# Six weight slots in place of four, three units held for both token tiles at the borders of stages, and loops written out, in a two-block transformer kernel

## The chip, the cores and the metric

The program runs on one core of a Trainium2 chip. The metric is the device time of one execution in microseconds (us), the median over several runs. The engines are TensorE (PE, with its weight loads PEld), VectorE (DVE), ScalarE (ACT), GpSimd (POOL) and the queue of SyncE (SP), which only issues transfers here.

## What is computed

256 tokens of width 1024 pass through two transformer blocks, all in float32. Cut to what matters here:

```python
# first block
proj = x @ w_in                                # q, k, v, g, p: 5 x 512 columns
ret  = rms(retention(rope(q), rope(k), v)) * silu(g)
mix  = concat([ret, pool_mixer(p)]) @ w_out
x = layernorm(ALPHA * x + mix)                 # ln1
u = x @ w_up                                   # 2 x 2816 columns
x = layernorm(ALPHA * x + (silu(conv3(gate)) * val) @ w_down)      # ln2
# second block
x = x + 0.5 * rmsnorm(swiglu(rmsnorm(x), ffn1_w_in, ffn1_w_down))
h = rmsnorm(x)                                 # mix_pre
q_a, f_a, i_a, g_a, q_b, k_b, v_b, f_b, gates = split(h @ w_in_2)
y = gate0 * (hgrn2(...) @ w_branch_a) + gate1 * (fox_attention(...) @ w_branch_b)
x = x + rmsnorm(y @ w_out_2)
x = x + rmsnorm(mem_cross_attention(rmsnorm(x), rmsnorm(mem)))
x = x + 0.5 * rmsnorm(swiglu(rmsnorm(x), ffn2_w_in, ffn2_w_down))
```

## The kernel before

**Products.** A weight matrix is streamed from HBM in units of 1 MB: 128 partitions x 2048 float32, which is 4 row chunks of 512 columns. Each float32 number is held as two parts, `high` (rounded by ACT, line 1066) and `rest` (raw minus high, by DVE, line 1538), both fp32r. One product is then three matmuls (high x high, high x rest, rest x high; lines 587 to 589 in `unit`, 624 to 626 in `by_tiles`). There are two token tiles of 128 tokens; a unit has 4 chunks, so 12 matmuls for each tile, 24 in all. There are 180 units, in the order of `BLOCKS`: win1, wout1, up1, down1, upA, downA, win2, brA, brB, mk, wout2, mv, mq, mo, upB, downB. `UNIT[name]` is the number of the first unit of a stage. An up block is two units and fills one PSUM pair; a down stage is 11 units that all add to both pairs.

**Slots.** `raw`, `high` and `rest` have 4 slots of 8 KB per partition each, 96 KB together. Unit u uses slot u % 4. SP loads unit u once DVE has made the rest of unit u - 4 (`unit_rest`); ACT may write `high` of unit u once PE is done with unit u - 4 (`unit_used`). ACT and DVE are in-order queues: where they convert units is fixed in the program by `split_to(n)`, which converts all units below n that aren't converted yet. In the inner blocks it stands at `2 * j + 4`.

**Borders.** At four borders a stage's input comes from a norm over the output of the stage before: wout1 to up1 (called x1 below, a layernorm), down1 to upA (f1, a layernorm), downA to win2 (m2, an RMS norm) and mo to upB (f2, an RMS norm). The last two units of the stage before are multiplied tile by tile (`by_tiles`): first both units for tile 0, which then signals `tile_done`, then both for tile 1, so the norm of tile 0 runs while PE works on tile 1. `first_block` does the same with the first two units of the next stage: it transposes tile 0 on PE in two groups of four (called q0 and q1, line 699, written to PSUM), ACT rounds each group to `xt_high` (line 1080), DVE subtracts to `xt_rest` (line 1556), and PE multiplies tile 0 by both units while the norm of tile 1 is made on DVE and ACT. Then the same for tile 1.

**Names of DVE's steps.** Layernorm: `layer_stats` (line 1644 adds, 1655 and 1657 take the moments, tile 1 needs all of the stage's products) and `layer_norm` (lines 1583, 1663, 1665; with a next gain also 1601); its root is ACT's `layer_root` (line 1117). RMS norm: ACT's `post_norm` takes squares of the stage's output (lines 1151, 1170, 1155, root 1117), DVE's `post_norm` (lines 1583, 1612, 1619, 1601) the rest. At x1 and f1 DVE makes the second `xt_rest` group of tile 0 inside the chain of tile 1, between its moments and its root.

**Loops.** On PE, ACT, DVE and SP, pairs of up blocks, and SP's loads of down stages, are a loop over a register (`turns.loop`). The rest is straight code.

Of the kernel before, what the change touches and what calls it, by code (L numbers as in the profile page):

```python
# [38 lines left out]
P = 128  # L39
# [15 lines left out]
SLOTS = 4  # L55
# [34 lines left out]


class Turns:

    def __init__(self, engine):
        self.engine, self.turn = engine, None

    def __call__(self, n, more):
        return n if self.turn is None or more == 0 else self.turn * more + n  # L100

    @contextmanager
    def loop(self, times, *counts):

        before = [c[0] for c in counts]
        with self.engine.Fori(0, times) as turn:
            self.turn = turn
            yield
            self.turn = None
        for c, n in zip(counts, before):  # L110
            c[0] += (c[0] - n) * (times - 1)

PAIRS = (FB - 1) // 2
CONV_PAIRS = PAIRS - 1


def two_on(key):  # L120
    return key[0], key[1] + 2
# [28 lines left out]
def aux_plan():  # L150
# [36 lines left out]
    for u in range(36):  # L187
        j, last = u // 2, u % 2 == 1
        if u == 1:
            use(("flog", 0))  # L190
# [46 lines left out]
def build(nc, dram, out_dram):  # L237
    ctx = ExitStack()
    with ctx:
# [20 lines left out]
        high = place("high", [P, SLOTS, 4 * NB], F32R, base + 32 * KB)  # L260
        rest = place("rest", [P, SLOTS, 4 * NB], F32R, base + 64 * KB)
# [183 lines left out]
        def _(sync):  # L445
# [3 lines left out]
            turns = Turns(sync)  # L449
# [17 lines left out]
            def load_up(u, w, j):  # L467

                wv = w.rearrange("(k p) n -> p k n", p=P)
                for half in range(2):  # L470
                    k = 4 * half
                    load(u + half, lambda d: [(d.rearrange("p (k g n) -> p k g n", k=4, g=2)[:, :, g, :],
                                               wv[:, k:k + 4, bass.ds(turns(g * FF + 256 * j, 512), 256)])
                                              for g in range(2)])

            def load_down(u, w, i):

                load(u, lambda d: [(d[:, k * D:(k + 1) * D], w[bass.ds(turns((2 * i + k) * P, SLOTS * 2 * P), P), :])
                                   for k in range(2)])

            for name, k in BLOCKS:
# [11 lines left out]
                if name.startswith("up"):  # L493
                    load_up(u, w, 0)
                    with turns.loop(PAIRS):
                        for j in (1, 2):
                            load_up(u + 2 * j, w, j)
                    continue
                if name.startswith("down"):
                    with turns.loop(FB // SLOTS):  # L500
                        for i in range(SLOTS):
                            load_down(u + i, w, i)
                    for i in range(FB // SLOTS * SLOTS, FB):
# [14 lines left out]
        def _(pool):  # L518

            pool.wait_ge(unit_landed[SLOTS - 1], 32)  # L520
# [51 lines left out]
        def _(pe):  # L572
            done = [0]
            turns = Turns(pe)

            def unit(u, products, wait=None):
# [3 lines left out]
                if u:  # L580
                    pe.wait_ge(unit_rest, turns(u + 1, SLOTS))
# [19 lines left out]
            def wait_pair(name, j):  # L601
                n, used = PAIR[name, j]
                if used:
                    pe.wait_ge(pair_taken[n], turns(used, 1))
# [7 lines left out]
            def by_tiles(u, products, before=None, signal=False):  # L612


                for tt in range(TT):
                    for half in range(2):
                        slot = (u + half) % SLOTS
                        if tt == 0:
                            pe.wait_ge(unit_rest, u + half + 1)
                        if before:  # L620
                            before(tt, half)
                        for sh, sr, c, out, first, last in products(half, tt):
# [6 lines left out]
                        elif half == 1 and signal:  # L629
                            mm.then_inc(tile_done, 1)  # L630

            def first_block(name, key, src, ready):

                def before(tt, half):
                    if half == 0:
# [3 lines left out]
                        if tt == 1:  # L639

                            wait_pair(name, 0)
                    wait_taken((key, 2 * tt + half))

                by_tiles(UNIT[name], lambda half, tt: chunk_products(name, 0, half, tt), before)
# [7 lines left out]
            def last_halves(name):  # L652

                by_tiles(UNIT[name] + 2, lambda j, tt: chunk_products(name, j, 1, tt), signal=True)

            def last_block(name, j):
                wait_pair(name, j)
                by_tiles(UNIT[name] + 2 * j, lambda half, tt: chunk_products(name, j, half, tt), signal=True)
# [9 lines left out]
            def down(name, i):  # L668
# [4 lines left out]
                if i < FB - 2:  # L673
                    unit(UNIT[name] + i, [p for kc in (2 * i, 2 * i + 1) for tt in range(TT)
                                          for p in down_products(i, kc, tt)])
                elif i == FB - 1:
                    by_tiles(UNIT[name] + i - 1,
                             lambda half, tt: [p for kc in (2 * (i - 1 + half), 2 * (i - 1 + half) + 1)
                                               for p in down_products(i - 1 + half, kc, tt)], signal=True)

            def aux(key):
# [3 lines left out]
                if used:  # L685
                    more = AUX[two_on(key)][2] - used if turns.turn is not None else 0
                    pe.wait_ge(aux_taken[bank], turns(used, more))
# [96 lines left out]
            def conv_transposes(j):  # L784
                pe.wait_ge(pair_taken[j % 2], turns(taken("up1", j)[1], 1))
# [4 lines left out]
            first_block("up1", "x1", from_x, lambda tt, q: pe.wait_ge(x_ready, x_at("ln1", tt, q)))  # L790
            full_block("up1", 1)
            conv_transposes(0)
            full_block("up1", 2)
            conv_transposes(1)
            with turns.loop(CONV_PAIRS, done):
                for j in (3, 4):
                    full_block("up1", j)
                    conv_transposes(j - 1)
# [7 lines left out]
            def ffn(u_name, d_name, h_name, key, pre):  # L806
                first_block(u_name, key, from_y, lambda tt, q: pe.wait_ge(normed, normed_at(pre, tt, q)))
                with turns.loop(PAIRS, done):
                    for j in (1, 2):
                        full_block(u_name, j)  # L810
                        hidden_transposes(u_name, h_name, j - 1)
# [6 lines left out]
            def hidden_transposes(u_name, h_name, j):  # L818
                n, count = taken(u_name, j)
                pe.wait_ge(pair_taken[n], turns(count, 1))  # L820
# [90 lines left out]
            for u in range(36):  # L911
                j, half = divmod(u, 2)
                if u == 0:
                    first_block("win2", "m2", from_y, lambda tt, q: pe.wait_ge(normed, normed_at("mix_pre", tt, q)))
                if u >= 2:
                    half_block("win2", j, half)
                if u in (1, 2):
                    fox_logits(u - 1)
# [121 lines left out]
        def _(act):  # L1040
# [3 lines left out]
            turns = Turns(act)  # L1044
# [8 lines left out]
            def split_to(n):  # L1053

                while split[0] < min(n, UNIT["end"]):
                    u = split[0]
                    act.wait_ge(unit_landed[u % SLOTS], turns(32 * (u // SLOTS + 1), 32))
                    if u >= SLOTS:
                        act.wait_ge(unit_used, turns(u - SLOTS + 1, SLOTS))
# [9 lines left out]
            def aux(key):  # L1069
                n, bank, _ = AUX[key]  # L1070
                more = AUX[two_on(key)][0] - n if turns.turn is not None else 0
                act.wait_ge(aux_done, turns(n + 1, more))
# [32 lines left out]
            def block_values(name, j):  # L1105
                act.wait_ge(unit_used, turns(filled(name, j), SLOTS))
# [116 lines left out]
            tile_groups("x1", 0)  # L1223
            layer_root("ln1", 1)
# [3 lines left out]
            def conv_values(j):  # L1228

                out = aux(("convg", j))  # L1230
                if j >= 2:
                    act.wait_ge(sem("ffn_rest"), turns(j - 1, 2))
                for c in range(2):
                    f = 2 * j + c
                    act.activation(conv[:, j % 2, c, :], out[:, c * S:(c + 1) * S], ACT.Identity,  # L1235
                                   scale=small["convw"][:, bass.ds(turns(3 * f + 2, 12), 1)],
                                   bias=small["convb"][:, bass.ds(turns(f, 4), 1)]).then_inc(sem("conv_last"), 1)
                act.wait_ge(aux_taken[6], turns(AUX["convg", j][2] + 1, 2))
# [952 lines left out]
```

## Time and profile before

| What | us |
|---|---|
| median of 3 runs | 1156.87 (1154.71 to 1157.2) |
| the profiled execution | 1158.97 |
| its span, first to last instruction | 1157.2 |
| PE busy | 1118.8 (97%) |
| PE weight loads | 933.2 (81%) |
| DVE busy | 690.4 (60%) |
| ACT busy | 562.6 (49%) |
| POOL busy | 42.5 (4%) |

The profile is of one execution. PE is busy in nearly the whole span, so the table tells little by itself; what is to be read is where PE stands still. The clock that TensorE was granted is 1.00 (2.4 GHz) or half of it (1.2 GHz), and its mean over the span is 0.995.

### The profile page before, as it was taken

How to read it: one execution, taken by the hardware profiler on the slowest of the kernel's cores; microseconds unless marked ns; L12 is line 12 of the kernel's file. 1: busy time of each engine (PE TensorE's matmuls, PEld its weight loads, DVE VectorE, ACT ScalarE, POOL GpSimd, SP SyncE). 2: the span in 40 equal slices, each digit the busy share in tenths (PEclk: the TensorE clock that was granted, in tenths of full speed). 3: DMA queues.
4: the chain of work that ended last, by engine and by line, in shares of the span. 5: the costliest groups of instructions: out<-in, count | busy, mean ns of one | idle time of the engine just before them, and what ended most of it. 6: DMA issues, size and time to landing. Idle time of an engine off the chain costs nothing.

```text
span 1157.2 us, 14090 instructions
## 1 busy us (share of the span) xinstructions
PE 1118.8 (97%) x5370; PEld 933.2 (81%) x5370; DVE 690.4 (60%) x682; ACT 562.6 (49%) x645; POOL 42.5 (4%) x50
## 2 busy tenths in 40 slices
PE   7999999999899999999999999999999899999997
PEld 5887888888788888878888888888888777888786
DVE  4548566665755545477976765667556347555442
ACT  4463556554363534466545545546355535435342
POOL 1900000000000000000000000010000000000000
PEclk9999999999999999999999999999999989999999
DMA  9645564547376555544543443464546233655530
GB/s 362 214 152 182 183 202 161 200 163 255 124 240 193 169 214 188 204 157 146 182 146 111 144 146 109 146 236 164 198 166 242 85 126 94 216 185 177 206 121 37
DMA packets 126145, 201.01 MB, mean 174 GB/s; under 512 B 6304, under 2 KB 74048, under 8 KB 125968
## 3 DMA queue, kind: packets, MB, share of 16 engines
q1 hardware_dynamic: 122624, 187.78, 47.3%
q0 software_dynamic: 3472, 12.55, 3.2%
q8 instruction: 34, 0.56, 0.2%
q14 instruction: 15, 0.12, 0.0%
HBM read 199.26 MB, written 1.05 MB: 173 GB/s over the span
## 4 chain that ended last, share of the span: by engine, by line
PE 91%; DVE 4%; ACT 2%; issue 2%; DMA 0%; SPq 0%; DVEq 0%; ACTq 0%
PE ps L587 24%; PE ps L589 24%; PE ps L588 24%; PE ps L699 4%; PE ps L624 3%; PE ps L625 3%; PE ps L626 3%; PE ps L857 2%; ACT high L1066 1%; DVE rest L1538 1%; PE ps L985 1%; PE ps L998 1%; DVE xt_rest L1556 1%; DMA x<-in_x_dram 0%; ACT xt_high L1080 0%
## 5 line engine op out<-in xcount | busy, mean ns | idle before, releaser
L1538 DVE TENSOR_TENSOR rest<-raw,high 128x2048 fp32r<-128x2048 f32 (+1 forms) x180 | 405.0, 2279 | 177.0 <-ACT high L1066 177.0
L587 PE MATMUL ps<-high,xt_high 128*128 128x512 f32 x928 | 369.7, 398 | 3.7 <-DVE rest L1538 2.1
L1066 ACT ACTIVATE high<-raw 128x2048 fp32r<-128x2048 f32 (+1 forms) x177 | 331.4, 1907 | 73.3 <-PE ps L589 72.5
L589 PE MATMUL ps<-high,xt_rest 128*128 128x512 f32 x928 | 363.8, 392 | 0.0
L588 PE MATMUL ps<-rest,xt_high 128*128 128x512 f32 x928 | 363.0, 391 | 0.0
L587 PEld LDWEIGHTS ps<-high,xt_high 128*128 128x128 f32 x928 | 175.5, 189 | 38.7 <-issue 2.5
L589 PEld LDWEIGHTS ps<-high,xt_rest 128*128 128x128 f32 x928 | 175.2, 189 | 37.6
L588 PEld LDWEIGHTS ps<-rest,xt_high 128*128 128x128 f32 x928 | 175.6, 189 | 34.9
L587 PE MATMUL ps<-high,ht_high 128*128 128x512 f32 x216 | 84.6, 392 | 2.5 <-issue 2.5
L589 PE MATMUL ps<-high,ht_rest 128*128 128x512 f32 x216 | 84.2, 390 | 0.0
L588 PE MATMUL ps<-rest,ht_high 128*128 128x512 f32 x216 | 84.0, 389 | 0.0
L1283 ACT ACTIVATE act<-ps,recips 128x256 f32<-128x256 f32 x44 | 18.5, 471 | 124.5 <-PE ps L589 124.5
L1779 DVE SCALAR_TENSOR_TENSOR hid<-ps,recips,act 128x256 f32<-128x256 f32 x44 | 19.3, 480 | 83.4 <-ACT act L1283 83.4
L1080 ACT ACTIVATE xt_high<-ps 128x512 fp32r<-128x512 f32 x38 | 21.2, 600 | 62.9 <-PE ps L699 62.9
L624 PE MATMUL ps<-high,xt_high 128*128 128x512 f32 x112 | 45.8, 409 | 5.1 <-DVE xt_rest L1556 5.0
L587 PEld LDWEIGHTS ps<-high,ht_high 128*128 128x128 f32 x216 | 40.5, 188 | 11.2 <-issue 3.1
L589 PEld LDWEIGHTS ps<-high,ht_rest 128*128 128x128 f32 x216 | 40.5, 188 | 8.6
L588 PEld LDWEIGHTS ps<-rest,ht_high 128*128 128x128 f32 x216 | 40.6, 188 | 8.3
L625 PE MATMUL ps<-rest,xt_high 128*128 128x512 f32 x112 | 45.1, 403 | 0.0
L626 PE MATMUL ps<-high,xt_rest 128*128 128x512 f32 x112 | 45.0, 402 | 0.0
L1556 DVE TENSOR_TENSOR xt_rest<-ps,xt_high 128x512 fp32r<-128x512 f32 x38 | 24.8, 684 | 21.9 <-ACT xt_high L1080 21.8
L1721 DVE SCALAR_TENSOR_TENSOR conv<-ps,convw,conv 128x255 f32<-128x255 f32 (+1 forms) x44 | 19.2, 478 | 20.7 <-ACT conv L1235 19.4
(304 smaller groups left out, 1168.0 us busy)
## 6 DMA issues: line engine op xcount, KB each, us to landing
raw<-in_w_in_dram SPq DMA_DIRECT2D x92, 512.0 KB, 4.2
raw<-in_ffn_w_in_dram SPq DMA_DIRECT2D x88, 512.0 KB, 4.7
raw<-in_w_up_dram SPq DMA_DIRECT2D x44, 512.0 KB, 4.7
raw<-in_ffn_w_down_dram SPq DMA_DIRECT2D x44, 512.0 KB, 4.1
raw<-in_w_down_dram SPq DMA_DIRECT2D x22, 512.0 KB, 4.7
raw<-in_w_out_dram SPq DMA_DIRECT2D x16, 512.0 KB, 4.3
raw<-in_w_mkv_dram SPq DMA_DIRECT2D x16, 512.0 KB, 5.1
raw<-in_w_branch_a_dram SPq DMA_DIRECT2D x8, 512.0 KB, 3.9
```

The costliest lines, as they stand in the source:

```text
L587: pe.matmul(out, sh, wh, start=first, stop=False)
L588: pe.matmul(out, sh, wr, start=False, stop=False)
L589: mm = pe.matmul(out, sr, wh, start=False, stop=last)
L624: pe.matmul(out, sh, wh, start=first, stop=False)
L625: pe.matmul(out, sh, wr, start=False, stop=False)
L626: mm = pe.matmul(out, sr, wh, start=False, stop=last)
L699: mm = pe.transpose(out[:, n * P:(n + 1) * P], src, ident[:, :])
L857: mm = pe.matmul(out[:, c:c + P // 2], hqk[:, h, t], q, start=True, stop=True)
L1066: act.activation(high[:, u % SLOTS, c], raw[:, u % SLOTS, c], ACT.Copy).then_inc(unit_high, 1)
L1080: act.activation(dst, src, ACT.Copy).then_inc(group_high, 1)
L1538: vec.tensor_tensor(rest[:, slot, c], raw[:, slot, c], high[:, slot, c].bitcast(F32), ALU.subtract).then_inc(sem("lead_rest") if lead else ...
L1556: vec.tensor_tensor(dst_rest, src, dst_high.bitcast(F32), ALU.subtract).then_inc(aux_taken[bank], 1)
```

## The change

`raw` and `rest` now share one place: DVE writes the rest over the raw data. With that there are 6 slots of 16 KB (raw/rest and high), 96 KB as before. A load of unit u now waits until PE is done with unit u - 6. `split_to` stands one unit further ahead (`+ 5`) in the inner blocks. At a border three units (`LEAD = 3`) are held for both tiles, before the border (down stages only) and behind it (`first_units`); at the ends of wout1 and mo it is still two. All loops over registers are written out. The forget-gate logits of win2 (`fox_logits`) come two units later.

```diff
-SLOTS = 4
+SLOTS = 6
+LEAD = 3
...
         raw = place("raw", [P, SLOTS, 4 * NB], F32, base)
-        high = place("high", [P, SLOTS, 4 * NB], F32R, base + 32 * KB)
-        rest = place("rest", [P, SLOTS, 4 * NB], F32R, base + 64 * KB)
+        rest = place("rest", [P, SLOTS, 4 * NB], F32R, base)
+        high = place("high", [P, SLOTS, 4 * NB], F32R, base + 48 * KB)
...
-                    sync.wait_ge(unit_rest, turns(u - SLOTS + 1, SLOTS))
+                    sync.wait_ge(unit_used, u - SLOTS + 1)
...
-            def first_block(name, key, src, ready):
+            def first_units(name, key, src, ready):
...
-                by_tiles(UNIT[name], lambda half, tt: chunk_products(name, 0, half, tt), before)
+                by_tiles(UNIT[name], LEAD, lambda n, tt: chunk_products(name, n // 2, n % 2, tt), before)
+                half_block(name, 1, 1)
...
-                if i < FB - 2:
+                if i < FB - LEAD:
...
-                with turns.loop(PAIRS, done):
-                    for j in (1, 2):
-                        full_block(u_name, j)
-                        hidden_transposes(u_name, h_name, j - 1)
+                hidden_transposes(u_name, h_name, 0)
+                for j in range(2, FB):
+                    full_block(u_name, j)
+                    hidden_transposes(u_name, h_name, j - 1)
...
                 def up_block(j):
-                    split_to(UNIT[u_name] + 2 * j + 4)
+                    split_to(UNIT[u_name] + 2 * j + 5)
...
             post_norm("ffn1_post", "downA", 0)
             first_group("m2")
+            split_to(UNIT["win2"] + LEAD)
             post_norm("ffn1_post", "downA", 1)
             other_groups("m2")
...
             layer_norm("ln1", 0)
-            tile_groups("x1", 0, halves_=(0,))
+            tile_groups("x1", 0)
+            split_to(UNIT["up1"] + LEAD)
             layer_stats("wout1", 1)
-            tile_groups("x1", 0, halves_=(1,))
             layer_norm("ln1", 1)
             tile_groups("x1", 1)
```

On DVE at the border x1, from the last step of tile 0's norm to tile 1's, before:

```order
L1665 SCALAR_TENSOR_TENSOR x<-y,recips,gains 128x512
L1556 TENSOR_TENSOR xt_rest<-ps,xt_high 128x4x128
L1644 SCALAR_TENSOR_TENSOR y<-x,ps 128x512 x2
L1655 BN_STATS moments<-y 128x6 x2
L1657 BN_AGGR meanvar<-moments 128x2
L1556 TENSOR_TENSOR xt_rest<-ps,xt_high 128x4x128
L1583 RECIPROCAL recips<-roots 128x1
```

and in the changed kernel (line numbers shift; 1619 is the old 1665, 1493 the old 1538, 1598 the old 1644):

```order
L1619 SCALAR_TENSOR_TENSOR x<-y,recips,gains 128x512
L1510 TENSOR_TENSOR xt_rest<-ps,xt_high 128x4x128 x2
L1493 TENSOR_TENSOR rest<-raw,high 128x2048
L1598 SCALAR_TENSOR_TENSOR y<-x,ps 128x512 x2
L1609 BN_STATS moments<-y 128x6 x2
L1611 BN_AGGR meanvar<-moments 128x2
L1537 RECIPROCAL recips<-roots 128x1
```

The second `xt_rest` group moved ahead of tile 1's first step, and one conversion of 128x2048, that of the third unit, now stands between them.

On ACT at the border m2, from the rounding of q0 of tile 0, before:

```order
L1117 ACTIVATE roots<-sums,eps 128x1
L1080 ACTIVATE xt_high<-ps 128x4x128
L1151 ACTIVATE y,eps<-ps 128x512
L1170 ACTIVATE y,sums<-ps 128x512
L1155 ACTIVATE eps<-eps 128x1
L1117 ACTIVATE roots<-sums,eps 128x1
L1080 ACTIVATE xt_high<-ps 128x4x128 x3
```

and in the changed kernel:

```order
L1076 ACTIVATE roots<-sums,eps 128x1
L1039 ACTIVATE xt_high<-ps 128x4x128
L1026 ACTIVATE high<-raw 128x2048
L1110 ACTIVATE y,eps<-ps 128x512
L1129 ACTIVATE y,sums<-ps 128x512
L1114 ACTIVATE eps<-eps 128x1
L1076 ACTIVATE roots<-sums,eps 128x1
L1039 ACTIVATE xt_high<-ps 128x4x128 x3
L1026 ACTIVATE high<-raw 128x2048
```

ACT's half of the third unit's conversion (`high<-raw`) stands behind q0 and ahead of tile 1's squares, and q1 of tile 0 (the first of the last `xt_high` three) is still behind those squares. At f2 the order is the same; at x1 and f1 both groups of tile 0 come first, then the conversion.

## Rows read from the trace of the kernel before

**Rows 1.** Page: costliest groups (busy, mean ns, idle before) and one DMA issue (KB, us to landing).
```profile
L1538 DVE TENSOR_TENSOR rest<-raw,high 128x2048 fp32r<-128x2048 f32 (+1 forms) x180 | 405.0, 2279 | 177.0 <-ACT high L1066 177.0
...
L1066 ACT ACTIVATE high<-raw 128x2048 fp32r<-128x2048 f32 (+1 forms) x177 | 331.4, 1907 | 73.3 <-PE ps L589 72.5
...
raw<-in_w_up_dram SPq DMA_DIRECT2D x44, 512.0 KB, 4.7
```

**Rows 2.** Windows, end of the old stage to tile 1's first product: x1, f1, m2, f2.
```profile
106.06:116.47 10.41, 8.14 (x41) 6.08 (x40) 8.94 (x16) 2.96 (x6) 1.05 (x2) 1.00 0.03 9
301.26:313.99 12.73, 9.80 (x41) 7.34 (x41) 11.58 (x19) 2.59 (x6) 1.75 (x4) 0.87 0.04 6
494.85:505.60 10.75, 8.08 (x41) 6.21 (x41) 8.61 (x15) 4.20 (x11) 1.06 (x2) 1.00 0.09 29
959.13:968.82 9.69, 8.09 (x41) 6.14 (x40) 7.49 (x12) 3.58 (x10) 0.00 (x0) 1.00 0.00 0
```

The columns are the window and its length, then busy us and count of PE, PEld, DVE, ACT and POOL, the granted clock, the DMA share and GB/s.

**Rows 3.** Timeline of PE at x1, tile 0 (start, us, instruction, idle before).
```profile
107.33 0.66 PE L699 MATMUL ps<-ident,x 128*128 128x128 f32 x4 [0.68 <-DVE x L1665]
108.07 0.50 PE L624 MATMUL ps<-high,xt_high 128*128 128x512 f32 x1
```

**Rows 4.** Timeline of DVE at x1: tile 1's chain, first and last.
```profile
107.93 1.27 DVE L1644 SCALAR_TENSOR_TENSOR y<-x,ps 128x512 f32<-128x512 f32 x2
...
113.74 0.75 DVE L1665 SCALAR_TENSOR_TENSOR x<-y,recips,gains 128x512 f32<-128x512 f32 x1
```

**Rows 5.** Timeline of PE at f1, tile 0.
```profile
304.13 0.65 PE L699 MATMUL ps<-ident,y 128*128 128x128 f32 x4 [1.57 <-DVE y L1601]
...
304.73 0.54 PE L624 MATMUL ps<-high,xt_high 128*128 128x512 f32 x1
```

**Rows 6.** Timeline of DVE at f1: tile 1's chain, first and last.
```profile
304.59 1.28 DVE L1644 SCALAR_TENSOR_TENSOR y<-x,ps 128x512 f32<-128x512 f32 x2
...
312.05 0.69 DVE L1601 TENSOR_TENSOR y<-x,gains 128x512 f32<-128x512 f32 x1
```

**Rows 7.** Timeline of PE at m2: tile 0's first product, tile 1's transposes.
```profile
497.88 0.50 PE L624 MATMUL ps<-high,xt_high 128*128 128x512 f32 x1
...
503.50 1.07 PE L699 MATMUL ps<-ident,y 128*128 128x128 f32 x8
```

**Rows 8.** Timeline of PE at f2: tile 0's first product.
```profile
961.14 0.50 PE L624 MATMUL ps<-high,xt_high 128*128 128x512 f32 x1
```

**Rows 9.** Timeline of ACT at f2: tile 1's squares, then q1 of tile 0.
```profile
960.26 0.59 ACT L1151 ACTIVATE y<-ps 128x512 f32<-128x512 f32 x1
...
961.94 0.58 ACT L1080 ACTIVATE xt_high<-ps 128x512 fp32r<-128x512 f32 x1
```

**Rows 10.** Timeline of DVE at f2: q1 of tile 0, tile 1's chain, first and last.
```profile
962.55 0.69 DVE L1556 TENSOR_TENSOR xt_rest<-ps,xt_high 128x512 fp32r<-128x512 f32 x1 [1.46 <-ACT xt_high L1080]
963.16 0.15 DVE L1583 RECIPROCAL recips<-roots 128x1 f32<-128x1 f32 x1
...
967.11 0.69 DVE L1601 TENSOR_TENSOR y<-x,gains 128x512 f32<-128x512 f32 x1
```

**Rows 11.** Timeline of PE inside mo, ahead of a stretch at clock 0.5.
```profile
923.17 1.06 PE L699 MATMUL ps<-ident,mo 128*128 128x128 f32 x8 [0.90 <-issue]
925.86 0.47 PE L587 MATMUL ps<-high,xt_high 128*128 128x512 f32 x1 [1.62 <-DVE xt_rest L1556]
```

**Rows 12.** Timeline of PE in upA: transposes behind three blocks one after another.
```profile
341.81 0.60 PE L699 MATMUL ps<-ident,hid 128*128 128x128 f32 x4
...
353.16 0.60 PE L699 MATMUL ps<-ident,hid 128*128 128x128 f32 x4
...
364.53 0.60 PE L699 MATMUL ps<-ident,hid 128*128 128x128 f32 x4
```

**Rows 13.** Timeline of PE: first product of downA, behind the loop.
```profile
434.40 0.47 PE L587 MATMUL ps<-high,ht_high 128*128 128x512 f32 x1 [1.09 <-issue]
```

**Rows 14.** Timeline of DVE at the same place: it empties the last pair.
```profile
433.42 0.88 DVE L1779 SCALAR_TENSOR_TENSOR hid<-ps,recips,act 128x256 f32<-128x256 f32 x2 [4.22 <-ACT act L1283]
```

More of the change, by code:

```diff
@@ L89 @@
 OA_SLOT = {30 + _g: _g for _g in range(4)}
[L92 to L121, printed above, removed]
 def unit_starts():
@@ L493, in _ @@
                 if name.startswith("up"):
[L494 to L497 removed]
+                    for j in range(FB):
+                        load_up(u + 2 * j, w, j)
                     continue
                 if name.startswith("down"):
[L500 to L503, printed above, removed]
+                    for i in range(FB):
                         load_down(u + i, w, i)
@@ L610, in half_block, with by_tiles @@
                 unit(UNIT[name] + 2 * j + half, [tiles[tt][k] for k in range(4) for tt in range(TT)])
-            def by_tiles(u, products, before=None, signal=False):
+            def by_tiles(u, units, products, before=None, signal=False):
                 for tt in range(TT):
-                    for half in range(2):
-                        slot = (u + half) % SLOTS
+                    for n in range(units):
+                        slot = (u + n) % SLOTS
                         if tt == 0:
-                            pe.wait_ge(unit_rest, u + half + 1)
+                            pe.wait_ge(unit_rest, u + n + 1)
                         if before:
-                            before(tt, half)
-                        for sh, sr, c, out, first, last in products(half, tt):
+                            before(tt, n)
+                        for sh, sr, c, out, first, last in products(n, tt):
                             wh, wr = high[:, slot, c:c + NB], rest[:, slot, c:c + NB]
@@ L685, in aux @@
                 if used:
-                    more = AUX[two_on(key)][2] - used if turns.turn is not None else 0
-                    pe.wait_ge(aux_taken[bank], turns(used, more))
+                    pe.wait_ge(aux_taken[bank], used)
                 return ps[:, bank, :]
@@ L1070, in aux @@
                 n, bank, _ = AUX[key]
-                more = AUX[two_on(key)][0] - n if turns.turn is not None else 0
-                act.wait_ge(aux_done, turns(n + 1, more))
+                act.wait_ge(aux_done, n + 1)
                 return ps[:, bank, :]
@@ L1249, in up1_block @@
                     conv_values(j - 1)
-            up1_block(0)
-            up1_block(1)
-            up1_block(2)
-            with turns.loop(CONV_PAIRS, split, steps):
-                up1_block(3)
-                up1_block(4)
-            split_to(UNIT["down1"] + 4)
+            for j in range(FB):
+                up1_block(j)
+            split_to(UNIT["down1"] + 5)
             conv_values(FB - 1)
@@ L1286, in up_block @@
                         hidden_high(j - 1)
-                up_block(0)
-                with turns.loop(PAIRS, split, steps):
-                    up_block(1)
-                    up_block(2)
-                split_to(UNIT[d_name] + 4)
+                for j in range(FB):
+                    up_block(j)
+                split_to(UNIT[d_name] + 5)
                 hidden_high(FB - 1)
@@ L1522, in settle @@
             def settle():
[L1523 removed]
+                vec.wait_ge(mine, steps[0])
             def split_to(n):
@@ L1543, in aux @@
                 n, bank, _ = AUX[key]
-                more = AUX[two_on(key)][0] - n if turns.turn is not None else 0
-                vec.wait_ge(aux_done, turns(n + 1, more))
+                vec.wait_ge(aux_done, n + 1)
                 return ps[:, bank, :]
@@ L1737, in up1_block @@
             def up1_block(j):
-                split_to(UNIT["up1"] + 2 * j + 4)
+                split_to(UNIT["up1"] + 2 * j + 5)
                 if j:
                     conv_values(j - 1)
-            up1_block(0)
-            up1_block(1)
-            up1_block(2)
-            steps_a_turn[0] = 6
-            with turns.loop(CONV_PAIRS, split, steps):
-                up1_block(3)
-                up1_block(4)
-            split_to(UNIT["down1"] + 4)
+            for j in range(FB):
+                up1_block(j)
+            split_to(UNIT["down1"] + 5)
             conv_values(FB - 1)
@@ L1785, in up_block @@
                         hidden_rest(j - 1)
-                up_block(0)
-                steps_a_turn[0] = 2
-                with turns.loop(PAIRS, split, steps, groups, silus):
-                    up_block(1)
-                    up_block(2)
-                split_to(UNIT[d_name] + 4)
+                for j in range(FB):
+                    up_block(j)
+                split_to(UNIT[d_name] + 5)
                 hidden_rest(FB - 1)
```

133 lines of the change are left out of this document (65 added, 68 removed).

## Prediction

> **What bounds the kernel now.** The first view is the page's table of engines: PE is busy for 97% of the span, and the number of matmuls does not change, so all that this change can move is the time in which PE stands still or runs at the lower clock. So the second view is the list of who PE waits for. It holds no row with a weight unit but one at the very start: PE never waits for a conversion in the middle of a stage, and four slots are already enough there. The waits stand at the borders of stages, behind norms, and inside the memory attention. So the third view is the timeline of PE, ACT and DVE at each of the four borders x1, f1, m2 and f2. The windows [rows 2] give the length of each, from the end of the old stage (called T) to tile 1's first product: 10.41, 12.73, 10.75 and 9.69 us, with PE busy for about 8 us of each. The reader is to see that DVE is busy in most of these windows too: in the first for 8.94 of 10.41 us, in the second for 11.58 of 12.73. The border is a chain of norms on DVE with PE as its customer, not the reverse.
>
> **A unit held for both tiles.** Three blocks of an up stage begin 11.35 and 11.37 us apart [rows 12], with four transposes (half of the 1.07 us of eight [rows 7], less their overlap: 0.45); four tile-units lie between, so a unit for one tile is 2.73 us of PE. Tile 0 then covers 8.2 us with three units instead of 5.5. The work is moved and not added. To compare, I let both kernels reach the same point: before, tile 1 starts with two units of tile 0 done, so the third adds 2.73 to its window.
>
> **What stands in tile 1's way.** The third unit has to be converted, and its place is the in-order queues of ACT and DVE ahead of tile 1's norm. ACT takes 1.91 us, DVE 2.28 [rows 1]. Its data is there: the slot was freed six units earlier, and a half of a unit lands in 4.7 us [rows 1]. But ACT comes to it only behind tile 0's `xt_high`, so DVE waits for ACT and then converts, in front of tile 1's chain.
>
> *x1.* T is 106.06. The last steps of tile 0 are as before: wout1 still ends with two units, q1 is transposed at 107.33 and the first product comes at 108.07, 0.74 later [rows 3]. ACT rounds q1 until 108.5, converts until 110.4; DVE converts until about 112.8. Tile 1's chain started at 107.93 before [rows 4], so it is 4.9 late; its last step ended at 113.74 + 0.75 = 114.5, now 119.4, and with 0.74 more tile 1's products start at 120.2, which is T + 14.1. Before, with the third unit added: 10.41 + 2.73 = 13.1. A loss of 1.0.
>
> *f1.* Here down1 ends with three units by tiles, so tile 0's norm starts 2.73 earlier. T is 301.26; the transposes of q1 came at 304.13 [rows 5], T + 2.9, now about T + 0.1. What is left is the way from both transposes to the product: at m2 503.50 to 505.60, so 2.1 [rows 7, 2]. Tile 0 starts at T + 2.1 and not at 304.73, T + 3.5 [rows 5]. ACT is free of `xt_high` at about T + 1.7, converts until T + 3.6, DVE until T + 5.9. Tile 1's chain takes 304.59 to 312.74, 8.15 [rows 6], so it ends at T + 14.0, and the products come at T + 14.8. Before: 12.73 + 2.73 = 15.5. A gain of 0.7.
>
> *m2 and f2.* Here ACT also has q1 of tile 0 behind tile 1's squares. Those take 960.26 to 961.94, 1.68 [rows 9]. From ACT's step behind q0, T + 1.1: 1.9 conversion, 1.7 squares, 0.6 rounding, 0.7 `xt_rest` [rows 10]: q1 is there at T + 6.0. PE wants it one unit behind its first product, which at f2 comes at 961.14, T + 2.0 [rows 8], so at T + 4.8: a new stop of 1.2. Then DVE converts until T + 8.3, its chain takes 963.16 to 967.80, 4.64 [rows 10], and with 0.74 tile 1 starts at T + 13.7. Before, f2: 9.69 + 2.73 = 12.4, a loss of 1.3. m2: tile 0's norm starts 2.73 earlier here too, its first product came at 497.88, T + 3.0 [rows 7], and comes at T + 2.1; but tile 1 starts at T + 13.7 as at f2, against 10.75 + 2.73 = 13.5: a loss of 0.2.
>
> Sum of the orders: 1.0 - 0.7 + 0.2 + 1.3 = 1.8 us of loss. Each border ends with DVE's conversion on the path; the bounds are 0 for it where it should fit into a hole (then the borders give -4.9, below) and its full length with ACT's, as here.
>
> **The clock.** The clock was granted at half in f1's window: its mean is 0.87, so 0.13 x 12.73 = 1.65 us of full-clock work were lost [rows 2]. What PE had done before: it stood from T to 304.73, 3.5 us with eight transposes in between [rows 5]. Inside mo it fell too, behind 922.27 to 925.86, 3.6 us with eight transposes [rows 11]. At m2, with 3.0 us of the same kind, and at x1 and f2, with 2.0, it stayed at 1.00 [rows 2, 3, 7, 8]. In f1 the loss was hidden: tile 1 waited for DVE anyway. Now the large holes lie behind tile 0's three units: at x1 from about 116.4 to 120.2, 3.8 us, at f1 from T + 10.4 to T + 14.8, 4.4 us, each with eight transposes. What follows them is 36 products with nothing to hide the slow ones, so each fall costs 1.65. By the nearest rows both are on the falling side; m2's 3.0 us is not far. I take 0.75 for f1 and 0.6 for x1: 1.35 x 1.65 = 2.2 us, between 0 and 3.3. The Trainium skill, TensorE: Matmul & The Clock Gate, Part 1, says that the lower clock is the default and that activity releases it. By that rule larger holes are a loss in themselves, and the trace agrees: the clock is at 0.5 behind the two longest holes quoted here; without it the sum would be 1.8, with it 4.0.
>
> **Slots, loads, loops.** In mid-stage a load waits for PE to finish unit u - 6 and lands 4.7 us later [rows 1], less than two units of 5.46 on PE; ACT could start on it only once PE had finished unit u - 4 before. So no conversion comes later, and as PE waited for none, none is worth anything earlier: 0. The cover is two units; were it gone, each unit would show its own wait. DVE writes over one of its operands now; no row here shows what that costs at this size. The nearest spread between two conversions of 128x2048 is DVE's 2.28 against ACT's 1.91 us [rows 1], so I bound it by 0.37 us either way at each of the four borders, where alone it is on the path (1.5 in all), and take 0, since operation and sizes stay. Loops: blocks of upA start 11.35 us apart once and 11.37 the next time, and one of these two steps has the loop's turn in it, since a turn is two blocks [rows 12], so a turn costs 0 within 0.02. The logits' move is PE work of the same length: 0.
>
> Sum: 1.8 + 2.2 = 4.0 us. The profiled execution took 1158.97 with a span of 1157.2; it is 2.1 above the median, a little more than one slow stretch of the clock. Added to the median 1156.87: **1160.9**.
>
> **Rivals.**
> *The third unit fits in* (faster). If DVE and ACT had the conversion done in idle time, tile 0's 8.2 us would cover most of tile 1's chain and each border would end on PE alone: T + 2.1 + 8.2 + 2.1 = 12.4. Against 13.1, 15.5, 13.5 and 12.4 that is -0.7 - 3.1 - 1.1 + 0 = -4.9 with f1's and x1's holes gone: 1152.0. For it speaks that tile 1's chain is only 4.6 us long at m2 and f2 [rows 10]; against it the order of the queues, and that DVE has hardly 1.5 us free at x1. It decides where the conversion costs a border less than about 1.2 us. 0.12.
> *Loops cost more than their turns* (no change). Downs start with a wait: 1.09 us at downA [rows 13], of which there are two like it. If that were code being fetched behind the loop, writing it out gives 2.2 us back: 1160.9 - 2.2 = 1158.7. Against it: DVE empties the last pair until 433.42 + 0.88 = 434.30, and the product comes at 434.40 [rows 13, 14]. That explains it whole. The Trainium skill, Runtime: NRT & Kernel Launch, Instruction fetch mechanics, says that a taken branch breaks the sequential prefetch and that kernels prefer full unrolling; by that rule this rival would win, and the trace does not agree, by the turns above. 0.08.
> *No clock falls* (no change). The holes stay but the clock holds: 1156.87 + 1.8 = 1158.7. For it: m2. 0.22.
> *Order and clock as summed*: 0.58, with one fall 1160.3, with both 1162.0.
>
> **Numbers.** 0.2% of 1156.87 is 2.3 us, about what a measurement of this kernel can tell from no change: slower is above 1159.2, faster below 1154.6. The first rival (0.12) is faster, and some 0.04 of the others, where my chains are two or three us too long. The middle two fall mostly within. The range leaves out the first rival and little above both falls: 1154.5 to 1163.5. The likeliest case alone: 1159.3 to 1163.
>
> **What would show it.** In the changed kernel, the conversion (128x2048 on DVE) directly ahead of tile 1's chain at each border; PE waiting 3 to 4 us ahead of tile 1 at x1 and f1 and about 1.2 ahead of the second unit of tile 0 at m2 and f2; tile 0's first product at f1 1.4 earlier; clock 0.5 behind the holes. Wrong would be: DVE finding the third unit converted, ACT reaching it before q0, a wait for a weight unit in mid-stage, or a stop where a loop used to be.

## The result, and the profile after

The changed kernel takes 1170.4 us in the median of 4 runs (1169.04 to 1171.12), the kernel before 1156.94 (1154.71 to 1157.2) beside it: a ratio of 1.0119 (95%: 1.0102 to 1.0137), 13.5 us slower. The sum was 4.0 us. The profiled execution took 1169.95 us with a span of 1167.8 and a mean clock of 0.992.

The page after, parts 1, 3 and 5: engines, one DMA queue, and the two groups that answer to [rows 1].

```profile
PE 1120.2 (96%) x5370; PEld 934.2 (80%) x5370; DVE 688.7 (59%) x682; ACT 561.0 (48%) x645; POOL 42.5 (4%) x50
...
q8 instruction: 43, 0.70, 0.2%
...
L1493 DVE TENSOR_TENSOR rest<-raw,high 128x2048 fp32r<-128x2048 f32 (+1 forms) x180 | 404.9, 2279 | 168.9 <-ACT high L1026 168.8
...
L1026 ACT ACTIVATE high<-raw 128x2048 fp32r<-128x2048 f32 (+1 forms) x177 | 330.9, 1907 | 44.7 <-DMA raw<-in_ffn_w_down_dram 22.3
```

The busy times are within 2 us of those of before, and a conversion that writes over the raw data takes the same 2279 ns. So the loss is idle time and clock. The windows of the four borders after, x1, f1, m2, f2, read as [rows 2]: from the end of the old stage to tile 1's first product.

```profile
104.55:118.86 14.31, 11.15 (x53) 8.65 (x52) 11.25 (x16) 3.89 (x5) 0.53 (x2) 0.96 0.37 124
301.93:316.57 14.64, 10.91 (x53) 8.65 (x52) 11.44 (x17) 3.78 (x5) 1.32 (x3) 0.97 0.38 130
495.89:509.61 13.72, 10.88 (x53) 8.34 (x52) 8.53 (x11) 5.41 (x11) 1.06 (x2) 1.00 0.36 131
968.40:982.12 13.72, 11.09 (x53) 8.32 (x52) 9.69 (x13) 5.42 (x11) 0.00 (x0) 1.00 0.38 127
```

They hold three units of tile 0 now. The prediction had 14.1, 14.8, 13.7 and 13.7. The borders came out as worked out, so most of the missing 9.5 us is elsewhere. It shows in the list of whom PE waits for (us in total, times, the longest):

```profile
...
PE ps L586 <- DVE xt_rest L1510: 6.3, 7, 1.6
PE ps L664 <- DVE y L1555: 4.5, 5, 1.6
PE ps L664 <- DVE flog L1857: 4.3, 1, 4.3
...
PE ps L664 <- DVE x L1619: 3.1, 3, 1.6
...
PE ps L884 <- DVE flog L1934: 1.9, 1, 1.9
```

Two of these rows are of no border: `flog`, the logits of the forget gate in win2, whose move the prediction had at 0. DVE's timeline in that place (start, us, instruction, idle before and its releaser):

```profile
524.67 2.29 DVE L1493 TENSOR_TENSOR rest<-raw,high 128x2048 fp32r<-128x2048 f32 x1
526.88 0.99 DVE L1889 TENSOR_SCALAR he<-ps,lb 128x256 f32<-128x256 f32 x2
533.30 1.00 DVE L1889 TENSOR_SCALAR he<-ps,lb 128x256 f32<-128x256 f32 x2 [5.44 <-PE ps L800]
534.44 0.69 DVE L1897 TENSOR_SCALAR hk<-he 128x1024 f32<-128x1024 f32 x1
...
543.18 0.22 DVE L1854 SCALAR_TENSOR_TENSOR flog<-ps,recips,flb 128x8 f32<-128x8 f32 x2
543.44 0.36 DVE L1857 SCALAR_TENSOR_TENSOR flog<-ps,recips,flog 128x8 f32<-128x8 f32 x2
```

DVE empties two groups of transposed `f` (line 1889). The first pair of steps goes through, the second stands 5.44 us and is released by line 800, which is the last matmul of the *logits*. And PE's:

```profile
525.02 1.09 PE L664 MATMUL ps<-ident,stage 128*128 128x128 f32 x8
525.86 0.48 PE L549 MATMUL ps<-high,xt_high 128*128 128x512 f32 x1
...
543.85 0.74 PE L664 MATMUL ps<-ident,stage 128*128 128x128 f32 x4 [4.34 <-DVE flog L1857]
...
558.87 0.38 PE L884 MATMUL ps<-ident,flog 128*8 128x128 f32 x2 [1.85 <-DVE flog L1934]
```

All eight transposes that DVE wants had been issued at 525.02. What holds DVE back is a count: every group in the four rotating PSUM banks adds 1 to one semaphore, `aux_done`, and a reader of group n waits for n + 1, in the order of `aux_plan`. The logits are one group written in two halves a unit of work apart. Before, its number and both halves came at steps 1 and 2, ahead of the transposes. In the change its number stands at step 3 ahead of those of `f`, but its second half is issued at step 4, behind them. So the second group of `f` is counted as there only when the logits are. DVE is late from then on and comes to `flog` only at 543.18; PE wants that bank for its next transposes and stands 4.34 us. DVE's small subtraction into `flog` (line 1934) is late as well: 1.85 us more. The clock falls behind the longer wait (windows after, columns as above):

```profile
540.00:544.00 4.00, 0.15 (x1) 0.15 (x2) 3.23 (x7) 2.57 (x3) 0.00 (x0) 1.00 0.71 258
544.00:548.00 4.00, 4.00 (x14) 3.23 (x14) 3.97 (x6) 3.04 (x5) 0.00 (x0) 0.57 0.00 0
```

That is 0.43 x 4.00 = 1.7 us, with the two waits 7.9 us, of the 9.5 that the sum missed. That is a reading; the runs below test it.

### The profile page after: what moved, and what is told of

Same layout as the page of the kernel before. It is cut to its first block, busy times and chain, and to the rows that moved or that the text cites. A ratio compares the mean times of both kernels' runs of the same rounds, so it can differ in the third digit from the quotient of the medians.

```text
span 1167.8 us, 13128 instructions
## 1 busy us (share of the span) xinstructions
PE 1120.2 (96%) x5370; PEld 934.2 (80%) x5370; DVE 688.7 (59%) x682; ACT 561.0 (48%) x645; POOL 42.5 (4%) x50
## 4 chain that ended last, share of the span: by engine, by line
PE 88%; DVE 5%; ACT 3%; issue 2%; DMA 0%; SPq 0%; DVEq 0%; ACTq 0%
PE ps L549 22%; PE ps L551 22%; PE ps L550 22%; PE ps L664 4%; PE ps L586 4%; PE ps L587 4%; PE ps L588 4%; PE ps L818 2%; ACT high L1026 1%; DVE rest L1493 1%; PE ps L946 1%; PE ps L959 1%; DMA x<-in_x_dram 0%; ACT xt_high L1039 0%; DVE xt_rest L1510 0%
## 5 line engine op out<-in xcount | busy, mean ns | idle before, releaser
L1493 DVE TENSOR_TENSOR rest<-raw,high 128x2048 fp32r<-128x2048 f32 (+1 forms) x180 | 404.9, 2279 | 168.9 <-ACT high L1026 168.8
L549 PEld LDWEIGHTS ps<-high,xt_high 128*128 128x128 f32 x896 | 169.1, 189 | 37.3 <-issue 2.5
L551 PEld LDWEIGHTS ps<-high,xt_rest 128*128 128x128 f32 x896 | 168.9, 188 | 36.2
L550 PEld LDWEIGHTS ps<-rest,xt_high 128*128 128x128 f32 x896 | 169.4, 189 | 33.5
L549 PE MATMUL ps<-high,ht_high 128*128 128x512 f32 x192 | 75.3, 392 | 2.6 <-issue 2.6
L551 PE MATMUL ps<-high,ht_rest 128*128 128x512 f32 x192 | 74.8, 390 | 0.0
L550 PE MATMUL ps<-rest,ht_high 128*128 128x512 f32 x192 | 74.7, 389 | 0.0
L549 PEld LDWEIGHTS ps<-high,ht_high 128*128 128x128 f32 x192 | 36.0, 188 | 10.5 <-issue 3.2
L551 PEld LDWEIGHTS ps<-high,ht_rest 128*128 128x128 f32 x192 | 36.0, 188 | 7.6
L550 PEld LDWEIGHTS ps<-rest,ht_high 128*128 128x128 f32 x192 | 36.1, 188 | 7.3
L586 PEld LDWEIGHTS ps<-high,xt_high 128*128 128x128 f32 x144 | 28.4, 197 | 14.5 <-DVE xt_rest L1510 4.8
```

The source lines that it names most:

```text
L549: pe.matmul(out, sh, wh, start=first, stop=False)
L550: pe.matmul(out, sh, wr, start=False, stop=False)
L551: mm = pe.matmul(out, sr, wh, start=False, stop=last)
L586: pe.matmul(out, sh, wh, start=first, stop=False)
L1493: vec.tensor_tensor(rest[:, slot, c], raw[:, slot, c], high[:, slot, c].bitcast(F32), ALU.subtract).then_inc(sem("lead_rest") if lead else ...
```

## The experiments

All ten kernels compute the same outputs: only the order of work changes. The first theory: logits about 8 us, borders 4 us with clock, the rest nothing. The rivals: the loops or slots cost, or the borders are worth more than their windows. The kernel before was measured again beside each group of runs, and its median came out between 1156.33 and 1157.3; so a difference of two medians from different groups is good to about 1 us.

**1. Logits moved, in the kernel before.**

```diff
-        if u == 1:
+        if u == 3:
             use(("flog", 0))
...
-                if u in (1, 2):
-                    fox_logits(u - 1)
+                if u in (3, 4):
+                    fox_logits(u - 3)
```

The steps of ACT and DVE that follow come two units later too, as in the change.

> The kernel before with only the logits moved two units later, as the change does it (halves on both sides of the first f transposes), four slots and loops as before. Theory of the count: DVE waits some 5 us for the second half here too, PE waits at the second f transposes and at the flog transposes: 5 to 8 us slower than before, 1162 to 1165. Rival (deeper conversions or slots are the cause): within 1 us of 1157.

Measured: 1163.94 us, ratio 1.0065 (1.0049 to 1.0081), +7.6 us. Its list of waits has the row that was to be explained:

```profile
PE ps L699 <- DVE flog L1910: 4.3, 1, 4.3
...
PE ps L923 <- DVE flog L1987: 1.8, 1, 1.8
```

and DVE stands in the same place, released by the last matmul of the logits (line 839 here):

```profile
529.60 1.00 DVE L1942 TENSOR_SCALAR he<-ps,lb 128x256 f32<-128x256 f32 x2 [6.16 <-PE ps L839]
```

The two waits and the fall of the clock behind them (1.7 us, at 540 to 546) make 7.8. Nothing else was changed, so this edit, in a kernel whose slots, borders and loops are those of before, makes the stop and most of the missing time. Shown.

**2. The halves together, in the changed kernel.**

```diff
-                if u in (3, 4):
-                    fox_logits(u - 3)
+                if u == 3:
+                    fox_logits(0)
+                    fox_logits(1)
```

> The changed kernel with both halves of the forget-gate logits ahead of the first f transposes, not one on each side of them. Theory (order of the count): the signal that a PSUM group is ready is one count for all groups in program order; in the changed kernel the logits' group is numbered ahead of the f transposes but finished one unit behind them, so DVE and ACT, which wait for the transposes' number, wait for the logits too (5.44 us on DVE), come late to the logits' bank and PE stands 4.34 + 1.85 us in the next two places. With both halves ahead these waits and the low clock behind them go: 6 to 8 us less than the changed kernel, 1162 to 1164. Rival (the deeper conversions, one unit further ahead, hold ACT and DVE up in win2): the waits stay, within 1 us of 1170.

Measured: 1166.38 us, ratio 1.0092 (1.0076 to 1.0108), 4.0 less than the change; 6 to 8 had been expected. The stop of 4.34 is gone, so the count was its cause, but less comes back than stop and clock together (6.0). The windows of this kernel around the logits (32 matmuls of 16 and 8 columns, 524.05 to 527.54):

```profile
526.00:530.00 4.00, 4.00 (x28) 3.71 (x28) 3.46 (x5) 0.26 (x1) 0.00 (x0) 0.81 0.64 243
530.00:534.00 4.00, 4.00 (x15) 3.15 (x15) 2.74 (x6) 2.97 (x4) 0.00 (x0) 0.76 0.00 0
```

PE is busy for 4.00 of 4.00 us, and still the clock falls behind the logits: (0.19 + 0.24) x 4.00 = 1.7 us. One repair brought a loss of its own.

**3. Halves apart, numbered and issued behind the transposes.**

```diff
-        if u == 3:
-            use(("flog", 0))
...
                 use((WIN2[j - 1][0] + "T", 2 * ((j - 1) % 2) + g))
+        if u == 3:
+            use(("flog", 0))
```

On PE, the call of `fox_logits` is placed behind the transposes of the same step.

> The changed kernel with the logits numbered and issued behind the first f transposes, one half there and one half a unit later. Theory: the count is in order again, so the 4.34 us wait goes as in the run with both halves together, and as the two halves of small matmuls are a unit apart the clock, which fell behind them there though PE stood nowhere, stays up: 2 us less than that run's 1166.4, 1163.5 to 1165. Rival (the clock fell for another reason, such as its phase): equal to it within 0.8 us.

Measured: 1164.6 us, ratio 1.0064 (1.005 to 1.0078), 5.8 less than the change. No stop at the transposes and no fall behind the logits; but the second wait is now 2.6 us, and the clock falls behind that one:

```profile
PE ps L882 <- DVE flog L1934: 2.6, 1, 2.6
```

The time is in the range that was expected, but not for the reason given there. Against experiment 2 the trace has as many falls of the clock in win2, one, and a second wait that is 0.8 us longer (2.6 for 1.8). What its trace has less is one fall inside mo, where the two programs are alike. That the halves apart are worth 1.8 us is not shown by this run; experiment 10 asks it again.

**4. Logits repaired whole, borders as in the change.** As 3, and DVE's subtraction into `flog` stands ahead of the conversions of its step:

```diff
+                if u == 6:
+                    vec.wait_ge(sem("flog_ln"), 1)
+                    vec.tensor_tensor(flog[:, :, :], flabs[:, :, :], flmin[:, :, :], ALU.subtract).then_inc(sem("flog_ready"), 1)
                 split_to(UNIT["win2"] + u + 5)
```

> The changed kernel with the logits repaired in full (behind the first f transposes, halves a unit apart, small subtraction ahead of the conversion) and the borders left as the change has them. This measures the sum of the prediction by itself: orders at the borders 1.8 us of loss and two clock falls of 1.65 at x1 and f1, 1160 to 1162.5 against 1157 of before. Rival (the four borders cost more than their orders, since the run with the early third unit gained 9.3 us, more than the 6.7 plus 3.3 summed for it at the low end): 1163 or more. Rival (less than predicted): under 1159.

Measured: 1161.41 us, ratio 1.0041 (1.0026 to 1.0057), +4.2 us. This is the kernel that the prediction had summed: 4.0 above the median, and inside its range. PE's waits at the borders are those of the change:

```profile
PE ps L586 <- DVE xt_rest L1510: 6.3, 7, 1.6
PE ps L664 <- DVE y L1555: 4.5, 5, 1.6
...
PE ps L664 <- DVE x L1619: 3.1, 3, 1.6
```

Of `flog` one wait of 0.4 is left.

**5. Loops written out alone, in the kernel before.**

```diff
-                with turns.loop(PAIRS, done):
-                    for j in (1, 2):
-                        full_block(u_name, j)
-                        hidden_transposes(u_name, h_name, j - 1)
+                for j in range(1, FB):
+                    full_block(u_name, j)
+                    hidden_transposes(u_name, h_name, j - 1)
```

and so for every other loop over a register on PE, ACT, DVE and SP.

> The kernel before with all register loops written out and nothing else. Theory: the turns cost nothing before and longer code costs nothing: within 1 us of 1157. Rival (longer code has to be fetched in order and PE or SP waits for it): 1 to 4 us slower. Rival (a loop's turn or end costs time): 1 to 3 us faster, with the waits of 1.1 us ahead of the down stages gone.

Measured: 1157.04 us, ratio 1.0003 (0.9992 to 1.0014). No difference that can be told.

**6. Slots and loops alone.** The change with `LEAD = 2` and the logits in their old place.

> The changed kernel with two units held at the borders and the logits in their old place: what is left is six slots with the rest over the raw data, loads that wait for PE, conversions one unit further ahead, and loops written out. Theory: these parts are worth nothing, within 1.2 us of 1156.3. Rival (writing over an operand or the later loads cost): 1158 or more. Rival (deeper slots help by themselves): 1155 or less.

Measured: 1158.12 us, ratio 1.0006 (0.9997 to 1.0015). Six slots, the rest over the raw data, the split one unit further ahead and the written-out loops together are within what can be measured. The 1158.12 is above what was expected and just inside the rival's "1158 or more", but the kernel before stood at 1157.3 beside it and not at 1156.3: the difference is 0.8 us, at most 1.7 by the interval. No wait for a weight unit is in its list but the one at the start.

**7. The third unit converted earlier, in the change.** DVE is idle ahead of tile 0's norm at x1, by its timeline after:

```profile
99.31 1.29 DVE L1598 SCALAR_TENSOR_TENSOR y<-x,ps 128x512 f32<-128x512 f32 x2 [3.34 <-PE ps L588]
```

3.34 us would take a conversion of 2.28. At f1, m2 and f2 DVE's last idle time ahead of tile 0's norm is 4.02, 4.77 and 6.19 us. So at all four borders, on ACT and DVE:

```diff
-            split_to(UNIT["up1"] + 2)
+            split_to(UNIT["up1"] + LEAD)
             layer_stats("wout1", 0)
```

> The changed kernel with the third unit converted ahead of tile 0's norm at all four borders, where its slot is long free, not between the norms of tile 0 and tile 1. Theory (the conversion stands on tile 1's chain): x1 1.7, f1 2.4, m2 1.3, f2 1.3 us less, and the clock falls of x1 and f1 go: 7 to 10 us below the changed kernel, 1160 to 1163.5; the logits' waits stay. Rival (DVE and ACT are late at the borders for another reason, such as the loads' later start): under 2 us.

Measured: 1161.14 us, ratio 1.0049 (1.0034 to 1.0063), 9.3 less than the change, with both faults of the logits still in it.

**8. The same with the logits repaired whole** (7 and 4 together).

> Both repairs: the third unit converted ahead of tile 0's norm, the logits behind the first f transposes and a unit apart, and the one small subtraction for the flog transposes moved ahead of the conversion of its step. Theory: 1161.1 of the run with the early third unit, less 4.3 and 1.4 us of waits and one or two clock stretches of 1.7: 1152 to 1154.5, faster than the kernel before (1156.3) by 0.2 to 0.4%. Rival (a remaining loss of its own in the deeper slots): 1156 or more.

Measured: 1150.89 us in the median of 5 runs (1150.35 to 1153.35), ratio 0.9945 (0.9931 to 0.9958): 6.4 us faster than before, and 1.1 below the range that was expected. The profiled execution is the slowest of the five, 1153.35. Its windows at x1, f1 and f2 and DVE's step ahead of tile 0's norm at x1:

```profile
104.55:116.98 12.43, 10.61 (x53) 8.42 (x52) 9.17 (x16) 2.95 (x6) 1.05 (x2) 1.00 0.47 160
298.96:311.37 12.41, 10.77 (x54) 8.41 (x52) 10.39 (x17) 2.38 (x5) 1.54 (x3) 1.00 0.45 153
953.14:965.55 12.41, 10.59 (x54) 8.42 (x52) 7.63 (x13) 4.18 (x11) 0.00 (x0) 1.00 0.41 143
```

```profile
99.31 1.28 DVE L1598 SCALAR_TENSOR_TENSOR y<-x,ps 128x512 f32<-128x512 f32 x2 [1.10 <-PE ps L588]
```

The conversion takes 2.2 us out of a hole, and tile 0's norm starts at 99.31 in both. The windows are 1.9, 2.2 and 1.3 us shorter than after's, and the clock is 1.00 in them. m2 goes from 13.72 to 12.84, by PE's timeline:

```profile
489.58 0.60 PE L664 MATMUL ps<-ident,y 128*128 128x128 f32 x4
...
502.42 0.47 PE L586 MATMUL ps<-high,xt_high 128*128 128x512 f32 x1 [1.07 <-DVE xt_rest L1510]
```

**9. Earlier at x1 and f1 only.** As 8, with m2's and f2's third conversion between the tiles as in the change.

> As the best run so far, but with the third unit converted early only at the two layernorm borders x1 and f1; at m2 and f2 it stands between the tiles as in the changed kernel. Theory: m2 loses 1.3 and f2 1.3 us again and no clock falls there, so 2.5 to 3 us above the 1150.9 of the best run: 1153 to 1154.5. Rival (the RMS borders hide it): within 0.8 us of 1150.9.

Measured: 1153.73 us in 10 runs, ratio 0.9976 (0.9964 to 0.9987), 2.8 above 8. By the windows m2 and f2 are worth 0.9 + 1.3 = 2.2, but the two profiled executions are nearly alike, 1153.83 and 1153.35. The clock makes that up. Inside mo, where the code is the same and PE stands 0.90 and 1.62 us on either side of eight transposes in both traces, it fell in kernel 8's trace and held in this one's (this kernel's window, then kernel 8's):

```profile
920.00:924.00 4.00, 3.52 (x16) 2.94 (x17) 3.00 (x3) 3.16 (x2) 0.00 (x0) 1.00 0.00 0
```

```profile
920.00:924.00 4.00, 4.00 (x11) 3.20 (x12) 3.11 (x2) 2.66 (x2) 0.00 (x0) 0.58 0.00 0
```

That is 0.42 x 4.00 = 1.7 us, and 2.2 - 1.7 = 0.5, the difference of the two. So medians and windows agree that m2 and f2 want the early place too.

**10. As 8, with both halves of the logits in one place**, behind the transposes.

> As the run with both repairs, but both halves of the logits in one place behind the first f transposes. Theory (32 matmuls of 8 or 16 columns in a row, 3.6 us, bring the clock down although PE is busy in every row): clock 0.5 behind them for about 3.4 us, 1.7 us slower than the run with the halves apart. Rival (only time without matmuls brings it down): equal within 0.8 us, clock 1.00 there.

Measured: 1153.71 us, ratio 0.9963 (0.9949 to 0.9977), 2.8 above 8. The windows of this kernel around the logits:

```profile
516.00:520.00 4.00, 4.00 (x37) 3.87 (x35) 4.00 (x4) 1.88 (x2) 0.00 (x0) 1.00 0.59 188
520.00:524.00 4.00, 4.00 (x18) 3.38 (x19) 2.74 (x6) 1.99 (x2) 0.00 (x0) 0.75 0.21 80
524.00:528.00 4.00, 4.00 (x16) 3.17 (x15) 1.98 (x4) 3.99 (x5) 0.00 (x0) 0.82 0.00 0
```

and of kernel 8, the halves a unit apart:

```profile
516.00:520.00 4.00, 4.00 (x32) 3.69 (x31) 4.00 (x5) 1.64 (x2) 0.00 (x0) 1.00 0.65 209
520.00:524.00 4.00, 4.00 (x19) 3.31 (x18) 2.74 (x5) 2.22 (x2) 0.00 (x0) 1.00 0.16 58
524.00:528.00 4.00, 4.00 (x27) 3.57 (x27) 1.99 (x4) 3.99 (x5) 0.00 (x0) 1.00 0.60 190
```

Same work, PE busy throughout in both; with the small matmuls together the clock is lower by (0.25 + 0.18) x 4.00 = 1.7 us. The 2.8 between the medians is less firm: five executions each, and the two intervals overlap a little.

## Why the prediction was wrong

The step that failed is one line: "The logits' move is PE work of the same length: 0." The length was right and the order was not looked at. It is worth 7.6 us alone (experiment 1) and 1170.4 - 1161.41 = 9.0 on top of the rest of the change (experiment 4). Of the 9.0 the trace shows 7.9: 4.34 and 1.85 of waiting and 1.7 of clock; less the 0.4 that experiment 4 still waits, about 1.5 stay unplaced. Part of that may be chance: the trace of the change loses 3.4 us to the clock inside mo (952 to 962 us), that of experiment 4 loses 1.7, in the same code. The two orders of the instructions on PE would have shown it blind: the second half of the logits behind eight transposes, its number ahead of them.

Point by point:

- *The borders' orders, a loss of 1.8.* Right. Against the old windows with 2.73 for the third unit (13.1, 15.5, 13.5, 12.4) the new ones give +1.2, -0.9, +0.2 and +1.3 = 1.8. Tile 0 at f1 starts 2.0 behind the border (2.1 was said), and at m2 and f2 PE stands 1.02 and 1.03 us ahead of tile 0's second unit (1.2 was said). PE's busy time in the old window of f1 was 9.80 us and not about 8, but no sum used it.
- *The clock, 2.2 between 0 and 3.3.* It fell behind both of the large holes, at x1 and f1, and at m2 and f2 it held; the likelier side was right at all four. It fell at x1 and f1 in all four traces with these borders (the change, experiments 2, 3 and 4). But the two rows that the prediction rested on, the holes of 3.5 us at f1 and 3.6 in mo with eight transposes, looked surer in one trace than they are: the same hole at f1 was followed by a fall in the kernel before and experiment 6 and by none in experiments 1 and 5, and the one in mo by a fall in 5 of the 12 traces. What each costs is what was said: 0.30 and 0.13 of two windows of 4 us at x1, so 1.7. Part of it lies ahead of tile 1's products; experiment 4 has orders and clock together at 4.2, for 4.0 summed.

Windows after, behind the hole of x1:

```profile
116.00:120.00 4.00, 2.56 (x11) 2.14 (x12) 2.74 (x5) 1.35 (x3) 1.05 (x2) 0.70 0.09 20
120.00:124.00 4.00, 4.00 (x17) 3.25 (x16) 2.89 (x3) 3.45 (x2) 0.00 (x0) 0.87 0.76 243
```

- *Slots, loads, in place: 0.* Right (experiment 6, and 2279 ns as before).
- *Loops: 0.* Right (experiment 5). The instruction queue moves 0.70 MB instead of 0.56, and no time goes with it. The Trainium skill, Runtime: NRT & Kernel Launch, Instruction fetch mechanics, prefers full unrolling; at ratio 1.0003 the runs don't bear that out here.
- *The rival that the third unit fits in.* It was not what this kernel does, but the sum worked out for it, 4.9 below the median, is close to what the same units give in the right place: 6.4 below before. From experiment 6 to 8, three units held for both tiles are worth 7.2 us, with the repaired move of the logits in it. With the windows alone, experiment 8 has 12.43 + 12.41 + 12.84 + 12.41 = 50.1 where the old ones with the third unit have 54.5: 4.4 less, for 4.9 in the rival's sum. The prediction held against it that "DVE has hardly 1.5 us free at x1", which was read in the window behind the old stage's end; it did not look ahead of tile 0's norm, where 3.34 us were free.
- *The range's upper end, 1163.5*, came from two falls of the clock. It had no case for a stop that the change makes outside the borders.

From experiment 4 to 8 the time falls by 10.5 us between the medians, and by 8.0 between the spans of the profiled executions (1159.2 and 1151.2). The windows account for 1.9 + 2.2 + 0.9 + 1.3 = 6.3, the two falls' parts behind the windows for 1.1 and 1.3, and the last wait on `flog` for 0.4, 9.1 in all; the fall in mo that the trace of 8 has and that of 4 has not takes 1.7 back, which leaves 7.4 for 8.0. The other 2.5 between the medians lie in executions without a trace and are not placed.

So the change joins a good step in the wrong place with a harmful one: three units held, with the conversion ahead of tile 0's norm, are a gain; the logits' move, as it is made here, takes more than that away. The six slots alone gave nothing, and whether three units could be held on four was not run.

## What to carry to other kernels

Where one semaphore counts groups in program order, a piece of work is not moved alone: check at which instruction each number is signalled, and who waits for a later one. An equal amount of work in a new place can be put at 0 only once the order of the signals has been looked at on the engine that makes them and on those that wait. A conversion that a new scheme needs belongs in the last hole before the chain that bounds the border: here 3.34 us were free ahead of the first tile's norm at x1, and the move there was worth 9.3 us over four borders in the change (experiment 7) and 10.5 between experiments 4 and 8, of which the traces show 8.0. And where a stretch at the lower clock costs 1.7 us and comes and goes in the same code, two traces are compared stretch by stretch before a difference of that size is given to an edit.

## What the runs showed of the hardware

The clock fell without PE standing still. In experiments 2 and 10, 32 matmuls of 16 and 8 columns follow one another for 3.5 us with PE busy in every row, eight transposes directly behind or ahead of them, and the granted clock goes to 0.5 for a stretch behind them; with 16 and 16, a unit of work between, it stays at 1.00 behind them (experiments 3, 4, 8 and 9, and every other trace of this case: two against ten). The Trainium skill, TensorE: Matmul & The Clock Gate, Part 1, says that the clock is set by how busy PE has been; the busy time of these rows does not tell the two cases apart (4.00 of 4.00 us in both), so for these narrow matmuls the profile's busy share was no guide to the clock.

The same hole does not always bring the clock down. In mo PE stands 0.90 us, makes eight transposes, and stands 1.62 us, to the hundredth in all twelve traces of this case; the first time it does so the clock fell in 5 of them, the second time in 11. Each fall costs 1.7 us, and single traces of one kernel can differ by that.

An fp32 subtraction of 128x2048 that writes over one of its operands takes the same 2279 ns as into a place of its own.
